# Softmax queries and keys projected first and kept as rows, turned in the next stage; four running sequences attended to inside the projection

## What is computed

```python
xn = rms_norm(hp, norm1[l])
(gq, gk, gv, glog, gg), (dq, dk, dv) = mixer_inputs(xn, w_in[l], w_gk2[l], b_gk2[l], q_norm[l], k_norm[l])
# in mixer_inputs: dq, dk = rms_norm over groups of 64 columns, with q_norm and k_norm
o_gla, s_fin = gla_chunked(padf(gq), padf(gk), padf(gv), padf(glog), s0, GLA_CHUNK)
o_diff = diff_attn_prompt(dq, dk, dv, lam)          # causal, 1040 x 1040, 4 heads, 2 maps
hp = hp + merge_heads(o_gla, gg, o_diff, ...)
...
k_past = cache_k[page_table, :, l].reshape(DB, past, DIFF_HEADS, 2 * DIFF_DQK)
v_past = cache_v[page_table, :, l].reshape(DB, past, DIFF_HEADS, DIFF_DV)
o_diff_s = diff_attn_sample(dq, dk, dv, k_past, v_past, lam)
hs = hs + merge_heads(o_gla_s, gg, o_diff_s, ...)
...
hp = hp + hier_moe(rms_norm(hp, norm2[l]), ...)
```

## Time and profile before

| | us |
|---|---|
| median of 3 runs | 1950.88 |
| lowest, highest | 1946.66, 1960.76 |
| the profiled execution: its own time | 1954.16 |
| its span, first to last instruction | 1952.2 |
| projection, from the start to the mixers' first transfer | 484 |
| mixers, to the merge's first transfer | 597 |
| merge, experts and combination | 871 |

### The profile page before, as it was taken

The page is one execution under the profiler, slowest core; times in us unless marked ns, Lnnn a source line. Parts: engine busy times, 40 slices in busy tenths (PEclk is TensorE's granted clock), DMA queues, the critical chain, the costliest instruction groups (busy, mean ns, idle before and its releaser), DMA issues. The chain is left out here.

```text
span 1952.2 us, 37190 instructions
## 1 busy us (share of the span) xinstructions
PE 1633.7 (84%) x15031; PEld 1271.2 (65%) x15031; DVE 1284.1 (66%) x1692; ACT 853.6 (44%) x1357; POOL 402.5 (21%) x371
## 2 busy tenths in 40 slices
PE   5879899998478888688889499429999999999990
PEld 3747676786257777456667288417888888888870
DVE  6446442153668787679784554538888888988964
ACT  5331302222022322243434454127877877877850
POOL 0012122100213334233332000041022122222204
PEclk9979999999569999799999699659999999999995
DMA  9539699704858999999999423038999999999957
GB/s 334 183 122 355 230 351 364 253 28 145 332 195 345 384 370 421 365 331 384 364 359 375 140 100 151 22 152 323 397 401 407 409 400 405 404 403 405 402 210 277
DMA packets 109167, 585.71 MB, mean 300 GB/s; under 512 B 15248, under 2 KB 20752, under 8 KB 56048
## 3 DMA queue, kind: packets, MB, share of 16 engines
q0 software_dynamic: 47184, 304.44, 40.9%
q1 hardware_dynamic: 61856, 279.40, 36.6%
HBM read 537.80 MB, written 46.01 MB: 299 GB/s over the span
## 5 line engine op out<-in xcount | busy, mean ns | idle before, releaser
L2222 DVE TENSOR_TENSOR e_l<-first_w,e_h 128x1024 fp32r<-128x1024 f32 x256 | 294.9, 1218 | 10.4 <-ACT e_h L2219 10.1
L2219 ACT CAST e_h<-first_w 128x1024 fp32r<-128x1024 f32 x256 | 250.2, 1048 | 83.1 <-POOLq L2292 42.7
L375 DVE STREAM_TRANSPOSE d_ring<-d_ring 128x2048 f32<-128x2048 f32 x96 | 219.8, 2299 | 16.8 <-DMA d_ring<-in_cache_k,rows 16.3
L2181 PE MATMUL ps<-e_h,e_xh 128*128 128x512 f32 x512 | 207.2, 405 | 3.1 <-DVE e_xl L2231 3.1
L2183 PE MATMUL ps<-e_h,e_xl 128*128 128x512 f32 x512 | 204.2, 399 | 0.0
L2182 PE MATMUL ps<-e_l,e_xh 128*128 128x512 f32 x512 | 204.1, 399 | 0.0
L250 PE MATMUL ps<-d_ring,d_qb 128*32 128x128 f32 x3072 | 118.1, 303 | 87.8 <-DVE d_ring L375 87.4
L632 PE MATMUL ps<-wh,xh 128*128 128x512 f32 (+1 forms) x432 | 183.5, 425 | 6.2 <-DVE wl L867 6.2
L634 PE MATMUL ps<-wh,xl 128*128 128x512 f32 (+1 forms) x432 | 174.5, 404 | 0.0
L633 PE MATMUL ps<-wl,xh 128*128 128x512 f32 (+1 forms) x432 | 174.4, 404 | 0.0
L2299 POOL COPY e_row<-order 128x1 uint32 x32 | 80.7, 2523 | 424.2 <-PE ps L2189 418.1
(11 more groups left out here) (347 smaller groups left out, 3045.0 us busy)
## 6 DMA issues: line engine op xcount, KB each, us to landing
e_w<-in_w_down SPq DMA_DIRECT2D x32, 2048.0 KB, 8.8
first_w<-in_w_up SPq DMA_DIRECT2D x62, 1024.0 KB, 7.7
first_w<-in_w_gate SPq DMA_DIRECT2D x62, 1024.0 KB, 10.6
cat<-in_w_in SPq DMA_DIRECT2D x8, 2048.0 KB, 12.9
ys_d<-e_y SPq DMA_DIRECT2D x32, 512.0 KB, 10.0
ys_d<-cat POOLq DMA_DIRECT2D x1, 8192.0 KB, 32.5
kT<-in_x_prompt SPq DMA_DIRECT2D x8, 512.0 KB, 8.1
m_stage<-in_w_out SPq DMA_DIRECT2D x4, 1024.0 KB, 5.0
```

Of the source, the lines that this page charges most:

```text
L375: dve.transpose(self.in_ring((KEYS, b, g)), self.in_ring((KEYS, b, g))).then_inc(self.s_kt, 1)
L2181: pe.matmul(out, high, w_high, start=first, stop=False)
L2219: return act.copy(h13[:, :, kk, :], w13[:, :, kk, :])
L2222: return dve.tensor_tensor(l13[:, :, kk, :], w13[:, :, kk, :], h13[:, :, kk, :].bitcast(F32), ALU.subtract)
```

## The change

`EARLY` becomes 4. All nine tiles of dq are projected first, then all of dk, then dv, v, gate and qk: six passes of nine units, 54 as before. The x tiles, the low ranks and the decays now belong to the dq pass. The normalised queries are stored as rows in DRAM (`q_d`), the keys are stored as rows to their output anyway; only tile 0 is transposed in the projection. `WOVEN` is dv, v, gate, qk: 36 units instead of 27, for 136 slots instead of 72. The ring lies in `qT` and `kT` as before, which are not needed until the mixers. The load of the qk rows into `cat` moves from the projection's end to the mixers' start; that of the v rows stays, behind unit (qk, 1).

In the mixers, four sequences are left, 136 slots; the prompt steps keep their slots (96, 99, ..., 189), so the walk has 199 slots. The key rows come back in one transfer into `qT` (2 MB); one tile of them is transposed by PE in slot `lin_at[i]` + 6 and copied to `kT` by ACT in the next; as each tile is used, a tile of query rows is loaded into its place, and the eight are transposed in place at slots 92, 94, 96 and 98.

```diff
-EARLY = 2
+EARLY = 4
...
-    PASSES = [("dq", (0,)), ("dk", (0,)), ("v", EVERY), ("dv", EVERY), ("gate", EVERY), ("qk", EVERY),
-              ("dq", EVERY[1:]), ("dk", EVERY[1:])]
+    PASSES = [(name, EVERY) for name in ("dq", "dk", "dv", "v", "gate", "qk")]
...
-    WOVEN = [u for u, (_, name, _) in enumerate(UNITS) if name in ("dv", "gate", "qk")]
+    WOVEN = [u for u, (_, name, _) in enumerate(UNITS) if name in ("dv", "v", "gate", "qk")]
...
-                    elif name == "dk":
+                    elif name in ("dq", "dk") and (name, i) != ("dq", 0):
...
-                            sp.dma_start(k_rows[META + P * (i - 1):META + P * i], kn[:, n % 2, :]).then_inc(s_ko[n % 2], 16)
+                            to = k.q_d[i - 1] if name == "dq" else k_rows[META + P * (i - 1):META + P * i]
+                            sp.dma_start(to, kn[:, n % 2, :]).then_inc(s_ko[n % 2], 16)
...
-                        sp.dma_start(k.cat[0:T0, 0, 0:W], k.qk_d[0, 0:T0]).then_inc(s_back, 16)
-                        sp.dma_start(k.cat[:, 1:TILES, 0:W], k.qk_d[1:TILES].rearrange("i p n -> p i n")).then_inc(s_back, 16)
                         sp.dma_start(k.cat[:, 1:TILES, W:D], k.v_d[1:TILES].rearrange("i p n -> p i n")).then_inc(s_back, 16)
...
                 turn_x(0)
                 for u, (p, name, i) in enumerate(UNITS):
-                    if u == 1:
-                        turn_x(1)
-                    if name == "v":
-                        if i + 2 < TILES:
-                            turn_x(i + 2)
-                        elif i == TILES - 1:
+                    if p == 0:
+                        if i + 1 < TILES:
+                            turn_x(i + 1)
+                        else:
                             decays()
...
+                    elif (name, i) == ("dk", 2):
+                        pe.wait_ge(s_sp, 2)
+                        turn(TILES, SC)
+                    elif (name, i) == ("dk", 5):
                         new_scores()
-                    n = u - NO["dq", 1]
-                    if n >= 2:
-                        turn(n)
-                turn(len(QK) - 2)
-                turn(len(QK) - 1)
...
-                    if (name, i) == ("dv", 0):
+                    if (name, i) == ("dk", 0):
                         log_sigmoid()
...
+                sp.dma_start(k.cat[0:T0, 0, 0:W], k.qk_d[0, 0:T0]).then_inc(l_qk[0], 16)
+                sp.dma_start(k.cat[:, 1:5, 0:W], k.qk_d[1:5].rearrange("i p n -> p i n")).then_inc(l_qk[1], 16)
+                sp.dma_start(k.cat[:, 5:TILES, 0:W], k.qk_d[5:TILES].rearrange("i p n -> p i n")).then_inc(l_qk[2], 16)
                 for n, name in enumerate(("lam_q1", "lam_k1", "lam_q2", "lam_k2")):
                     sp.dma_start(lam4[:, n, :], io[name].to_broadcast([P, DK])).then_inc(a_lam, 16)
+                k_rows = io["k_prompt"].rearrange("a n l h d -> (a n) (l h d)")[META:META + SEQ]
+                sp.dma_start(k.qT[:], k_rows.rearrange("(i p) n -> p i n", p=P)).then_inc(a_k, 16)
...
+                for i in range(TILES - 1):
+                    sp.wait_ge(a_kt, i + 1)
+                    sp.dma_start(k.qT[:, i, :], k.q_d[i]).then_inc(a_q[i % 2], 16)
...
+                    pe.wait_ge(a_kk, i)
...
+                def turn_prompt_keys(i):
+                    pe.wait_ge(a_k, 16)
+                    pe.wait_ge(l_ok, i - 1)
+                    pe.wait_ge(l_end, min(i + 2, TILES))
+                    for h in range(HEADS):
+                        mm = pe.transpose(k.ps[:, LIN_OUT, h * P:(h + 1) * P], k.qT[:, i - 1, h * P:(h + 1) * P], ident)
+                    mm.then_inc(a_kt, 1)
...
+                        if i and after == 6:
+                            turn_prompt_keys(i)
...
-        k.kT, k.qT = sb("kT", [P, HEADS, META + SEQ]), sb("qT", [P, HEADS, SEQ])
+        k.kT, k.qT = sb("kT", [P, HEADS, META + SEQ]), sb("qT", [P, TILES - 1, W])
```

More of the change, by code:

```diff
@@ L492, in project, with rows_stored @@
         q_pad = [pieces[KEPT_P + j].rearrange("p (b h x) -> p b h x", b=SAMPLES // 2, h=HEADS) for j in range(2)]
+        def rows_stored(n, parity):
+            return sum((2 if QK[x] == ("dk", 0) else QK[x][1] > 0) for x in range(n + 1) if x % 2 == parity)
+        squared = k.cat[:, KD, 0:W]
         def slots_at(u, third):
@@ L816, in _ @@
                 high_w(0)
[L817 to L825 removed]
+                for i in range(1, TILES):
                     sum_squares(i)
@@ L891, in norm @@
                     dve.wait_ge(s_sq, n + 1)
-                    squared = (k.cat[:, KD, 0:W] if n < 2 else st[:, 0, :])[0:rows]
-                    chain.link(dve.reduce_sum(eight, squared.rearrange("p (g d) -> p g d", g=8), axis=X))
+                    chain.link(dve.reduce_sum(eight, squared[0:rows].rearrange("p (g d) -> p g d", g=8), axis=X))
                     dve.tensor_scalar(eight, eight, 1.0 / DK, EPS, ALU.mult, ALU.add).then_inc(s_s8, 1)
@@ L949, in new_rows, with keep_decays, finish_decays @@
                     chain.link(dve.memset(k.mt, 0.0))
+                def keep_decays():
+                    dve.wait_ge(s_gk, 48)
+                    for i in range(TILES):
+                        n = rows_of(i)
+                        dve.wait_ge(s_z, i + 1)
+                        dve.tensor_tensor(k.z[0:n, i, :], k.ps[0:n, 6 + i % 2, 0:GW], bgk[0:n], ALU.add).then_inc(s_zs, 1)
+                def finish_decays():
+                    dve.wait_ge(s_ln, 2)
+                    for rows, a, b in ((T0, 0, 1), (P, 1, TILES)):
+                        t = log_scratch[0:rows, a * GW:b * GW]
+                        z = k.z[0:rows, a:b, :].rearrange("p a n -> p (a n)")
+                        dve.scalar_tensor_tensor(out=z, in0=z, scalar=0.0, in1=t, op0=ALU.min, op1=ALU.subtract).then_inc(s_log, 1)
                 dve.wait_ge(s_gain, 16)
@@ L993, in _ @@
                                 r.vector_slot(dve, chain, n)
-                    if name in ("dq", "dk"):
-                        norm(QK.index((name, i)))
 def mixers(nc, k, io):
@@ L1018, in mixers @@
     STEP = [(i, h) for x in range(1, TILES // 2 + 1) for h in range(HEADS) for i in (TILES - x, x)]
+    Q_ORDER = [i for x in range(1, TILES // 2 + 1) for i in (TILES - x, x)]
+    Q_BANK = (5, 6, 5, 6, 6, 7, 6, 7)
     GROUPS_OF = {i: [list(range(0, i + 1))[a:a + 4] for a in range(0, i + 1, 4)] for i in range(1, TILES)}
```

230 lines of the change are left out of this document (111 added, 119 removed).

## The result

| | before, us | changed, us (forecast) |
|---|---|---|
| median (4 runs each) | 1950.95 | 2081.34 |
| lowest, highest | 1946.66, 1960.76 | 2070.99, 2087.54 |
| profiled execution: its own time | 1954.16 | 2080.74 (2041) |
| its span | 1952.2 | 2078.5 |
| first key tile on PE | 143.2 | 197.8 (180) |

The projection's end is taken 0.9 us ahead of the mixers' first transfer.

The account below looks back on a forecast made before the run. PE was taken to bound the woven pass and, in the mixers, engines waiting for each other; 1954 plus 114 in the projection less 27 in the mixers gave 2041, or 2038 on the median's scale, range 1985 to 2085.

Parts of the forecast that it names:

- Up to the first key tile: Start of the projection: first key tile on PE at 180 us instead of 143.25, +37; bounds 170 and 188.
- The 10 us ahead of the second set of transposes: In the dk pass, PE waits for the first key norm, queued behind log-sigmoid and page row numbers; about 10 us lost.
- the bubble of 11: PE's wait before the first key tile for last norm, row store, queries and one transpose; 11.29 us before the change.
- six periods: In the dq pass, six sets of x transposes at 7.1 us each, paced by ACT and DVE; set 8 at 73.
- The woven pass: Projection units with cache tiles: 410 us for 239, four buffers returning every 13.0 per key tile; bounds 378 and 450.
- PE's floor: PE's own work in the projection's units, cache tiles and turns, 378 us in total, 2.8 per slot.
- the mixed stretches: Three stretches of 26 mixed tiles at about 3.0 us and 6 value tiles at 2.75, together 284 us.
- PE does not keep the pass: Denies the rival that gathers land in 5.6 us, PE's 378 counts and the time is 2006; chance 0.16.
- The bare tail: Rival: the 18 last prompt steps run at DVE's 3.7 us each, 66 in all; time 1969, chance 0.09.
- Crowding: Rival: stores, weights and gathers fill DMA, landings of 10 us, 3.31 a slot, pass 450, time 2078; chance 0.08.
- The mixers up to step 13: Mixers' head: nothing shorter than 423 us; added 8 for the lambda vectors' wait and 5 for query loads, +13.
- Bare steps: The 18 mixer steps with no tile between: 6.8 us each, 122 instead of 151.5; chain 6.1 to 6.3, partly lower clock.

Follow-up runs that it names:

- The mended queue: Changed kernel with SP's first-pass queue re-ordered: four constant loads behind the fifth x tile, first two query stores ahead of the last x load and key weights; 2068.01 us, 1.0586.
- the filler: Changed kernel with nine 128 x 128 transposes added on PE in each prompt step behind the last gather, into an unused bank; 2052.49 us, 1.0481.

## Why the prediction was right, and what it missed

- **Up to the first key tile, +37 forecast, +55 measured.** The pace of 7.1 an x tile holds (sets at 28.20, 35.30, 42.55, 49.81). The 10 us ahead of the second set of transposes are 10.4, for the reason given, and the bubble of 11 is 9.9. What failed is the sentence that the chain through ACT and DVE sets the pace of *six periods*: after three of them the chain met the stores of the new query rows, which the prediction did not count. It asked of SP's queue only where the lambda vectors stand. The moved norms bring a store each, the store frees one of two buffers, and in the first pass SP's queue is full of loads; at the end of the projection, where these norms were, it had little else to do. The mended queue gives 181.2.
- **The woven pass, 410 forecast, 426 to PE's last matmul.** The mechanism fits the runs: PE's floor no longer holds (three sequences 328 by a formula that gives 331, four 51 over the same line), key tiles are late and value tiles are not, landings are 8.3, and a ring of three takes 485. The size was 4% short, and the term that was too small is the mixed stretches: from first matmul to first matmul, the 16 keys and the empty slots took 72.6 for 72, the three stretches of alternating tiles 104.9, 106.0 and 98.4 for 95 each and a part of the 12 for turns, the last values 42.2 for 44. With shares of 0.92, 0.97 and 0.98 the DMA engines alone were busy for 97, 103 and 97 us of these, more than the 95 that the buffers' cycle gave. The forecast counted 13.0 a key cycle at the median landing; landings up to 12.5 stand in it too. Whether late landings or full transfers make up the 16 us stays open. In the runs with this pass it took 414 to 426.
- **The rivals.** PE does not keep the pass: landings did not fall to 5.6. Its premise, that gathers queue only when the DMA is full, is not borne out either: with two sequences the landing was 6.8 at a share of 0.82. The bare tail does not run at DVE's 3.7 a step: with the clock at 0.99 a step takes 6.1. Crowding as it was put, landings of 10 us and 450 for the pass, did not come, though its time did. The shortest gather of the kernel before landed in 5.45 us, somewhat under the 5.6 that the prediction calls the least; which leaves its argument as it is.
- **The mixers up to step 13, +13 forecast, +11 measured** (+13 with two sequences). The sum is right, its parts are not: the lambda vectors' wait grew by 4, not 8. What delays the head is all that SP loads there; with the lambda vectors first, the query and key rows are waited for, 21 us. The two loaded ahead of the old states together bring step 0 from 313.4 to 301.3 (two sequences).
- **Bare steps, 6.8 forecast, 7.1 in the profiled execution, 7.6 to 8.0 in three others.** The chain's 6.1 to 6.3 was right, and 6.1 is what a step takes at the full clock. The clock was named, but under-sized: 0.5 to 0.7 us a step was allowed, 1.0 to 1.9 were needed. Over the four executions the 18 steps go with the clock: 128 us at 0.74, 136 at 0.68, 140 at 0.62, 144 at 0.60. The changed kernel's wider spread fits this (mean clock of the whole execution 0.893 at 2070.99 us, 0.881 at 2087.54), but only one of its runs has a profile. The 16 us behind the start of step 31 instead of 12 stand at a clock of 0.50; with the filler ahead of them, at 0.86, they are 12.9.
- **Where the move's gain went.** In the mixers a bare step is no shorter than one beside value tiles at the full clock: 7.1 to 8.0 us bare, 6.5 beside value tiles in the changed kernel, from step 8 to step 13. The stretch of these five steps, with a clock of 1.00:

```profile
1031.00:1064.00 33.00, 32.12 (x560) 22.55 (x558) 17.76 (x45) 13.79 (x39) 6.97 (x8) 1.00 0.68 258
```

  The tiles that were taken away kept PE busy, and beside them its clock was up. So the third sequence gives 28 back, the fourth 4, and two more only 36 together.
- **Its own signs.** Held: PE's idle of 10, landings of 8 to 9, steps 13 to 31 at 6.3 to 7.3 us in the profiled execution. Missed: first key tile by 188 (197.8), last value tile by 600 (622), the mixers' first transfer at 598 (629.5), the lambda vectors' wait near 20 (16.6).

## What to carry to other kernels

A step that is moved takes its stores along: look at what its store frees, how many buffers there are, and what stands in that queue at the new place. Work that fills a busy engine costs its own time up to the point at which a second bound (here the return of the four buffers, with the transfers nearly full beside it) is met, and more from there; find that point, and move only up to it. Taking work away beside a chain may lower the clock of the engine that the chain runs on, and give back nothing.

## What the runs showed of the hardware

The granted clock of PE fell to its lower level, 0.50, in bare steps, while others of the same kind ran at 1.00. Ahead of the step at 0.50 shown above, PE was busy 4.6 of 7.0 us, and its longest idle stretch was 1.82:

```profile
1089.00:1096.00 7.00, 4.58 (x20) 2.30 (x19) 2.82 (x7) 2.98 (x8) 0.00 (x0) 0.74 0.00 0
```

```profile
1095.96 1.71 PE L1310 MATMUL ps<-kT,qT 64*128 64x400 f32 x4 [1.82 <-ACT x_scratch L1466]
```

The mean of 18 such steps differs from execution to execution (0.60 to 0.74). With nine transposes of filler a step it is 0.99 from the third step with filler on. The Trainium skill (TensorE: Matmul & The Clock Gate, "A second HAM failure mode: psum-queue depth-cycling") tells of a kernel whose clock goes to and fro because of frequent short idles between groups of matmuls; this trace agrees, at a price of up to 2.3 us on a step of 6.2.

A gather of 64 rows into 64 partitions took 7.0 us where one of 128 rows took 8.3, and half the bytes kept the DMA engines busy nearly as long: 73.0% for 65 MB, 80.7% for 120. By these rows a packet took 0.46 us on average for 0.31 (share x 16 engines x 394 us / packets). The Trainium skill (SBUF — State Buffer, "Door 1: The DMA port swizzle (why `[64,N]` ≈ `[32,N]`)") states that partitions 0 to 63 reach 8 of the 16 ports of the local memory; the trace agrees with that, and no run here gathered into the other 64 partitions to test it.
